# First norm's modulation in columns, from row-wise pieces of the adaptive weights

## The reference, cut to what matters

```
mod = silu(c) @ w_ada + b_ada                 # c: 1024, w_ada: 1024 x 6144
sh1, sc1, gt1, sh2, sc2, gt2 = split(mod, 6)  # 1024 each
u = rmsnorm(x, norm_mix_g) * (1 + sc1) + sh1  # x: 512 tokens x 1024
z = u @ w_in                                  # to the RWKV part, the attention, the gates
... h = x + gt1 * (merged @ w_out) ...        # then norm, 32-expert MoE, final norm
```

## Time and profile before

| | us |
|---|---|
| median of 3 runs | 1351.78 (1351.62 to 1358.64) |
| the profiled execution's own time | 1352.31 |
| its span in the trace | 1350.6 |
| TensorE busy | 1123.2 (83%) |
| VectorE, ScalarE, GpSimd busy | 408.1, 217.7, 164.9 |
| TensorE's granted clock, mean | 0.925 |

### The profile page before, as it was taken

How to read it: one execution, slowest core, us unless ns; L and a number is a source line. 1 busy time by engine, 2 the same in 40 slices (tenths; PEclk the granted TensorE clock), 3 DMA queues, 4 the chain that set the end, 5 groups by cost and what they waited for, 6 DMA issues and landing times. The chain is left out here.

```text
span 1350.6 us, 16451 instructions
## 1 busy us (share of the span) xinstructions
PE 1123.2 (83%) x7001; PEld 572.5 (42%) x7001; DVE 408.1 (30%) x694; ACT 217.7 (16%) x443; POOL 164.9 (12%) x235
## 2 busy tenths in 40 slices
PE   2699999999997887989799992988887877777780
PEld 0343344544465555979644461333332333333330
DVE  4524436632004444345522336110001101111004
ACT  2101123220003452334200120000000000000002
POOL 1100001114001343214100001001000000000002
PEclk9999999879998998999999985988989899998985
DMA  9512326244224003300082445899999999999985
GB/s 341 214 66 94 119 99 242 103 169 125 101 94 133 1 1 120 140 2 4 1 319 110 199 170 216 355 428 427 430 429 429 429 430 429 428 431 428 430 344 202
DMA packets 61345, 311.87 MB, mean 231 GB/s; under 512 B 6194, under 2 KB 12676, under 8 KB 48728
## 3 DMA queue, kind: packets, MB, share of 16 engines
q1 hardware_dynamic: 49784, 273.79, 50.7%
q0 software_dynamic: 9184, 32.82, 6.3%
q10 hardware_dynamic: 2304, 4.20, 0.8%
HBM read 285.11 MB, written 24.64 MB: 229 GB/s over the span
## 5 line engine op out<-in xcount | busy, mean ns | idle before, releaser
L2272 PE MATMUL ps<-ring,zrT 128*64 128x512 f32 x704 | 168.7, 635 | 31.3 <-issue 28.4
L868 PE MATMUL ps<-ring,uT 128*128 128x512 f32 x384 | 169.5, 598 | 1.2 <-PE ps L868 0.6
L2292 PE MATMUL ps<-ring,hdT 128*64 128x512 f32 x352 | 122.2, 633 | 10.4 <-issue 8.5
L859 PE MATMUL ps<-uT,ring 128*128 128x512 f32 x256 | 113.9, 602 | 1.3 <-ACT uT L294 0.7
L2272 PEld LDWEIGHTS ps<-ring,zrT 128*64 128x64 f32 x704 | 57.7, 146 | 133.2 <-issue 132.8
L868 PEld LDWEIGHTS ps<-ring,uT 128*128 128x128 f32 x384 | 72.2, 191 | 92.9 <-issue 92.9
L2097 DVE TENSOR_TENSOR zrT<-zrT,ps 128x512 f32<-128x512 f32 x16 | 11.0, 687 | 290.0 <-PE ps L2272 290.0
L2272 PE MATMUL ps<-mg,zrT 128*64 128x512 f32 x160 | 75.7, 628 | 7.8 <-issue 7.8
L1920 ACT ACTIVATE zrT<-ps 128x512 f32<-128x512 f32 x16 | 9.6, 597 | 422.6 <-PE ps L2272 422.6
L859 PEld LDWEIGHTS ps<-uT,ring 128*128 128x128 f32 x256 | 48.4, 192 | 66.3 <-issue 65.2
L1854 POOL DMA_DIRECT2D y_dram<-zrT x16 | 9.1, 569 | 452.9 <-DVE zrT L2106 452.9
(11 more groups left out here) (365 smaller groups left out, 1478.4 us busy)
## 6 DMA issues: line engine op xcount, KB each, us to landing
ring<-in_moe_w_gate_dram SPq DMA_DIRECT2D x22, 2048.0 KB, 31.3
ring<-in_moe_w_up_dram SPq DMA_DIRECT2D x22, 2048.0 KB, 34.0
ring<-in_moe_w_down_dram SPq DMA_DIRECT2D x22, 2048.0 KB, 33.6
ring<-in_w_ada_dram SPq DMA_DIRECT2D x12, 2048.0 KB, 9.6
ring<-in_w_in_dram SPq DMA_DIRECT2D x9, 2048.0 KB, 13.8
mod<-in_moe_w_up_dram SPq DMA_DIRECT2D x5, 2048.0 KB, 31.5
mg<-in_moe_w_up_dram SPq DMA_DIRECT2D x5, 2048.0 KB, 30.9
uT<-in_moe_w_down_dram SPq DMA_DIRECT2D x5, 2048.0 KB, 36.5
```

The lines of the kernel that those rows point to most:

```text
L859: ins = pe.matmul(ps[:, n % 4, :], slot(name, KD, w)[:, k, c0:c0 + P], uT[:, k, :], start=(k == 0), stop=(k == KD - 1))
L868: ins = pe.matmul(ps[:, n % 4, :], uT[:, k, P * i:P * i + P], w, start=(k == 0), stop=(k == KD - 1))
L2272: ins = pe.matmul(ps[HALF * r:HALF * r + HALF, "gu".index(kind), :], xgT[:, b % 2, k, HALF * r:HALF * r + HALF], w[r][:, k, :], start=(k = ...
L2292: ins = pe.matmul(ps[HALF * r:HALF * r + HALF, 2 + c, :], hdT[:, j, HALF * r:HALF * r + HALF], w[r][:, j, 512 * c:512 * c + 512], start=(j ...
```

## The change

The order of loads is constants, `x`, then the ring. Units 0 to 3 are now two whole rows k of `w_ada` per partition (2048 columns, 8 KB each), each row a load of its own with its own semaphore; `zr0` comes in two halves of four k. VectorE multiplies a row by `silu(c)` and adds it to `acc1` (2048 columns wide): all of it for even k, only the shift half for odd k. The scale half of odd k goes to TensorE as stationary columns (`column_rows`), and the sums of `acc1` over the partitions too (`column_sums`): shift and scale come out as columns, one value per partition and k, in one PSUM bank. ScalarE scales `x` by the reciprocal root, TensorE transposes it before the modulation is known, and VectorE applies shift and scale to `uT` in place, one k at a time; the first z tile waits for each k.

```diff
-        ada_unit(u)
-    win_unit("zr0", 0, 512)
+        units.append((f"ada{u}", [(0, P, (1, 2 * D), ada[:, 2 * u + h:2 * u + h + 1, 0:2 * D]) for h in range(2)]))
+    units.append(("zr0", [(0, P, (4, 512), win[:, 4 * h:4 * h + 4, 0:512]) for h in range(2)]))
...
@@ SyncE
-                load_units(sp, 0, 2)
                 sp.dma_start(x, ...).then_inc(s_h, 16)
-                load_units(sp, 2, index["w1k"])
+                load_units(sp, 0, index["w1k"])
@@ GpSimd
-                pool.dma_start(grow[:, :], A["norm_mix_g"][0].partition_broadcast(P)).then_inc(s_small, 16)
+                pool.dma_start(gcol[:, :], A["norm_mix_g"][0].rearrange("(p k) -> p k", k=KD)).then_inc(s_small, 16)
+                pool.dma_start(bcol[:, :, :], A["b_ada"][0, 0:2 * D].rearrange("(s p k) -> p s k", s=2, k=KD))\
+                    .then_inc(s_small, 16)
@@ ScalarE
-                n1_root(act, 0, NT)
+                act.wait_ge(x_ms, 1)
+                act.activation(xrt, xms, ACT.Sqrt).then_inc(x_rt, 1)
+                act.wait_ge(x_rs, 1)
+                for i in range(NT):
+                    act.activation(x[:, i, :], x[:, i, :], ACT.Copy, scale=xrs[:, i:i + 1]).then_inc(x_sc, 1)
-                for u in range(4): ... copies of ps to mod
+                for n in range(2 * NT):  # then par
+                    act.wait_ge(x_T, n + 1)
+                    act.activation(uT[...], ps[:, n % 4, :]..., ACT.Copy).then_inc(x_ev, 1)
@@ VectorE
-                for u in range(4):
-                    ada(u)
...
+                for k in range(KD):
+                    dve.wait_ge(s_part[k], 16)
+                    w = slot(f"ada{k // 2}", 2, 2 * D)[:, k % 2, :]
+                    if k == 0:
+                        dve.tensor_scalar(acc1[:, :], w, csil[:, 0:1], None, ALU.mult).then_inc(s_ak, 1)
+                    else:
+                        n = D if k % 2 else 2 * D
+                        dve.wait_ge(s_ak, k)
+                        dve.scalar_tensor_tensor(acc1[:, 0:n], w[:, 0:n], csil[:, k:k + 1], acc1[:, 0:n], ...)
+                    if k == 1: ... mean of squares; wait for the root; reciprocal
...
+                dve.wait_ge(s_modp, 4)
+                link(dve.tensor_tensor(scol[:, :, :], ps[:, 4, 0:2 * KD]..., bcol[:, :, :], ALU.add))
+                link(dve.scalar_tensor_tensor(scol[:, 1, :], scol[:, 1, :], 1.0, gcol[:, :], ALU.add, ALU.mult))
+                dve.sem_inc(s_mod, 4)
+                dve.wait_ge(x_ev, 2 * NT)
+                for k in range(KD):
+                    dve.tensor_scalar(uT[:, k, :], uT[:, k, :], scol[:, 1, k:k + 1], scol[:, 0, k:k + 1], ALU.mult, ALU.add)\
+                        .then_inc(s_u1, 1)
@@ TensorE
+                def column(u, k, lhs, rhs, first, last):
+                    r = slice(HD * (u % 2), HD * (u % 2) + HD)
+                    return pe.matmul(ps[r, 4, KD * (u // 2) + k:KD * (u // 2) + k + 1], lhs, rhs, start=first, stop=last)
+                def column_rows(u):  # waits for s_part[2u+1]
+                    for k in range(KD):
+                        for h in range(2):
+                            ins = column(2 + h, k, w[:, D + 512 * h + k:D + 512 * h + 512:KD], csil[:, 2 * u + 1:2 * u + 2], ...)
+                def ada_back(u):     # waits for s_pk u+1 and s_ak 2u+2, gives the slot back
+                def column_sums(s_): # waits for s_ak 8-s_; 16 products of acc1 with a column of ones
-                for u in range(4): spread_mod(u)
+                for _ in range(6):
+                    pe.matmul(ps[:, 5, :], C("ident"), cst[:, 0:T], start=True, stop=True)
+                pe.wait_ge(s_csil, 1)
+                column_rows(0); ada_back(0)
                 pe.wait_ge(s_par, 96)
+                pe.wait_ge(x_sq, NT)
                 pe.transpose(ps[:, 6, 0:34], parr[:, :], C("ident")[0:34, 0:34]).then_inc(s_parT, 1)
-                for i in range(NT): n1_turned(pe, i)
+                x_turned(0); x_turned(1); column_rows(1); ada_back(1)
+                x_turned(2); x_turned(3); column_rows(2); ada_back(2)
+                column_sums(1); column_rows(3); column_sums(0); ada_back(3)
+                pe.wait_ge(x_ev, 2 * NT)
@@ first z tile
+                        if n == 0:
+                            pe.wait_ge(s_u1, k + 1)
+                            if k % 4 == 0:
+                                pe.wait_ge(s_part[2 * index["zr0"] + k // 4], 16)
```

More of the change, by code:

```diff
@@ L151, in build @@
     for n, (_, parts) in enumerate(units):
-        total[where[n]] += 16 * len(parts)
+        total[where[n]] += 16 * len(parts) if n >= FRONT else 0
         arrived.append(total[where[n]])
@@ L196, in build @@
         s_const = sem("s_const")
+        s_part = [sem(f"s_part{n}") for n in range(2 * FRONT)]
         def ring_slot(s_):
@@ L218, in load_units @@
                     eng.wait_ge(unit_free[where[n]], turn_of[n])
-                for p0, np_, (k, w), src in units[n][1]:
-                    eng.dma_start(ring_slot(where[n])[p0:p0 + np_, 0:k * w].rearrange("p (k n) -> p k n", k=k), src)\
-                       .then_inc(unit_in[where[n]], 16)
+                at_ = 0
+                for m, (p0, np_, (k, w), src) in enumerate(units[n][1]):
+                    landed = s_part[2 * n + m] if n < FRONT else unit_in[where[n]]
+                    eng.dma_start(ring_slot(where[n])[p0:p0 + np_, at_:at_ + k * w].rearrange("p (k n) -> p k n", k=k), src)\
+                       .then_inc(landed, 16)
+                    if n < FRONT:
+                        at_ += k * w
         def warm(pe, n=8):
@@ L336, in build @@
         bada = alloc(stage1, "bada", [12, 512])
+        bcol = alloc(stage1, "bcol", [P, 2, KD])
+        gcol = alloc(stage1, "gcol", [P, KD])
+        scol = alloc(stage1, "scol", [P, 2, KD])
+        n1s = alloc(stage1, "n1s", [P, 4, NT])
         uT = alloc(stage1, "uT", [P, KD, T])
@@ L385, in build @@
         junk1 = ps[:, 6:8, :].rearrange("p b n -> p (b n)")
-        n1_square, n1_mean, n1_root, n1_gain, n1_rows, n1_turned, n1_evacuate, _, n1_ev, _, _, _ = norm_mod(
-            stage1, "n1", x, u1, uT, grow, junk1, 0, 1, False)
+        s_ak, s_pk, s_csil = sem("s_ak"), sem("s_pk"), sem("s_csil")
+        acc1 = early[:, 0:2 * D]
+        x_sq, x_ms, x_rt, x_rs, x_sc, x_T, x_ev, s_u1 = (sem(f"x_{n}") for n in "sq ms rt rs sc T ev u1".split())
+        xss, xms, xrt, xrs = (n1s[:, n, :] for n in range(4))
         ztiles = [("T", f"zr{t // 4}", t, P * (t % 4)) for t in range(ZT_TILES)]
@@ L840, in side_job @@
                     ins.then_inc(w_job, 1)
-                for u in range(4):
-                    spread_mod(u)
+                for _ in range(6):
+                    pe.matmul(ps[:, 5, :], C("ident"), cst[:, 0:T], start=True, stop=True)
+                pe.wait_ge(s_csil, 1)
+                column_rows(0)
+                ada_back(0)
                 pe.wait_ge(s_par, 96)
+                pe.wait_ge(x_sq, NT)
                 pe.transpose(ps[:, 6, 0:34], parr[:, :], C("ident")[0:34, 0:34]).then_inc(s_parT, 1)
[L846 to L849, removed]
+                x_turned(0)
+                x_turned(1)
+                column_rows(1)
+                ada_back(1)
+                x_turned(2)
+                x_turned(3)
+                column_rows(2)
+                ada_back(2)
+                column_sums(1)
+                column_rows(3)
+                column_sums(0)
+                ada_back(3)
+                pe.wait_ge(x_ev, 2 * NT)
+                pe.wait_ge(s_small, 48)
                 pe.wait_ge(s_mod, 5)
                 for n, (kind, name, i, c0) in enumerate(ztiles):
-                    if name:
+                    if name and name != "zr0":
                         need(pe, name)
```

71 lines of the change are left out of this document (47 added, 24 removed).

## The result

| | before | after |
|---|---|---|
| median of four runs of each | 1355.21 us (1351.62 to 1362.19) | 1338.72 us (1337.81 to 1341.28) |
| ratio | | 0.987, 95% interval 0.984 to 0.990 |
| the profiled execution | 1352.31, span 1350.6 | 1341.28, span 1339.5 |
| z starts | 62.22 | 39.52 |
| TensorE's granted clock, mean | 0.925 | 0.91 |

Faster by 1.3%: 16.5 us between the medians, 13 to 22 us by the interval, 11.0 us between the two profiled executions. The forecast of 1331.6 was 7 us too low for the median, its range of 1325 to 1340 held it. At the start everything went better than forecast: z began 22.7 us earlier, where 20.2 were expected. So some of the 22.7 us is missing at the end: 11.6 between the two profiled executions, 6.2 between the medians.

A forecast was written before the change was run, and what follows sets the result against it. TensorE, idle for input until z at 62.22 us, was the bound; last sum 40.9, handovers 0.5 and first scaling 0.55 put z at 42.0, winning 20.2 us: 1331.6 us, own range 1325 to 1336, 8 in 10 for 1325 to 1340.

The forecast's parts named there:

- a batch: 16 fp32 one-column products (32 instructions) on TensorE in `column_rows` or `column_sums`: 2.2 us, bounds 1.4 to 4.0.
- the ring: Load slots that TensorE gives back: no gap for `ada3` or `zr0`; `zr1` at worst some 2 us late, free.
- GpSimd's moved loads: Eight transfers, 0.7 MB, now starting near 32 us: take up to 1.9 us from `zr0`, free by 4.5 us.
- dear batches: Column products on TensorE before z cost near 4.0 us a batch: z at 47 to 52, total 1337 to 1342; 13%.
- rival (d): One-column products into one bank don't overlap on TensorE: 7.7 us a batch, z at 70.1, total 1360; 4%.
- The last sum: End of sums(0) on TensorE, just ahead of z: taken as 40.9 us.
- the bound by data: Ahead of z, sums(1) not before k=6 is done at 33.4, then three batches: 40.0 us.
- The 2.8 us: A TensorE batch at the lower clock, if one-column products don't count as activity; z about 3 us later.
- a shift of that start should move everything behind it: From the first z product at 62.22 us products run almost without gap, so an earlier start moves all later stages.
- Rival (a): Column products dear or stalled by instruction loading in the first 40 us: z at 47 to 52, 1337 to 1342; 13%.
- Rival (c): Start is won but given back behind z by a later wait on an absolute time: 1347 to 1352 us; 6%.
- (b): Loads at the start pay a fixed time, 2.5 us each for four added: z at 50.4, total 1340; 4%.

The follow-up runs named there:

- side_by_side: Changed kernel with a batch's 64 stationary columns as memory neighbours instead of every eighth column, output not valid; 1341.26 us, one run.
- hold_z: Changed kernel with 22 chained VectorE copies ahead of the scaling of `uT`, delaying z; 1348.33 us, ratio 0.995 to the kernel before.
- hold_full: Changed kernel with 50 chained VectorE copies ahead of z, so z starts at 62.64; 1361.34 us, ratio 1.003 to the kernel before.
- keep_merge: Changed kernel with three unread TensorE products ending each of the two stages ahead of merge; 1333.34 us, ratio 0.985; repeated 1336.15 us, 0.986.
- x_late: Changed kernel with `x` loaded between `ada1` and `ada2` and the mean of squares after k=3; 1346.25 us, ratio 0.993 to the kernel before.
- before_keep: Kernel before the change with three unread TensorE products ending each of the two stages ahead of merge; 1355.11 us, ratio 1.000.
- keep_more: keep_merge plus two unread products ending the attention stage and one after `column_sums(0)`; 1335.76 us, ratio 0.986 to the kernel before.

## Why the prediction was right and where it was not

Right: that the start is the only thing won; that `x` lands near 13 (12.33); that VectorE would wait for DMA at each k, with additions of 1.285 and 2.35 us (1.28 and 2.35); k=7 at 33.6 (33.41); a batch at 2.2 us (2.09), between its bounds; the first z product inside 37.6 to 46 (39.52). That the ring and GpSimd's moved loads cost nothing held with little room: `zr0`'s first half, put at 36.3, landed at 37.9, 1.6 us before z, and at 39.4 in side_by_side. The DMA engines were full meanwhile (1.06 from 34 to 36 us), but at 342 GB/s, where 24 to 26 us have 426.

The total came inside the range in part by luck. The forecast's own range was 1325 to 1336, and 1338.72 lies above it, in the part that was added for dear batches, which did not come, and for scatter. The 7.1 us between 1331.6 and 1338.72 have three parts. The base was the median of three executions, 1351.78, and that of four is 1355.21: 3.4 us. The code behind z lost 6.2 us that the sum put at nothing, and the start won 2.5 more than forecast: 3.7 us. Where the chances are added up, 89, 7 and 5 make 101; rival (d) alone is 4.

Off in size, on the good side: z at 39.52 instead of 42.0. The last sum was priced at 40.9 and ended at 38.07 (36.01 + 2.06). `x` was scaled from 19.16 instead of 21.5 (`x` 0.7 us earlier, and ScalarE loaded its table at 17.04, before VectorE's mean, not behind it), so TensorE's queue was through in time and waited 0.89 us for VectorE's k=6. That left the bound by data, which the prediction put at 40.0 and which came 1.9 us lower: k=6 was added by 32.1 instead of 33.4, and the three batches behind it took 5.9 us instead of 6.6. The tail behind them was 1.45 us instead of 1.1. From 28 to 38 us, 8 us of that batches of one moving column, the clock is 0.50. By the Trainium skill's TensorE: Matmul & The Clock Gate, Part 1, activity releases the throttle; at these batches the trace shows no release. The 2.8 us that the prediction drew from it for a batch at the lower level was wrong: with the step of eight a batch takes 2.09 at either level.

Wrong: the first paragraph's step, "a shift of that start should move everything behind it". A shift does, as hold_z and hold_full show with 9.0 of 10.0 and 22.0 of 23.1. But the change is no shift alone. It adds instructions to TensorE, which puts a load boundary where it stalls (2.4 us, shown by the place that moves with the instruction count and by the load in the stall), and the merge stage then starts at the lower clock (4.0, shown by keep_merge). That is 6.4 us, and the medians lack 6.2. The rest of the 11.6 between the two profiles is about 1.5 in the chunk stage, 1.5 in the attention stage, 0.8 in the compression stage and 1.2 in z, all with a lower clock. It is not a fixed cost of the change: hold_full and x_late have the changed code without most of it, and before_keep has the part in z and compression without the change. Rival (a) named instruction loading for the first 40 us, where it did nothing visible; the stall sits 490 us further on. Rival (c) had part of the outcome at 6%: 6 us were given back, not nearly all, as its 1347 to 1352 has it, and not by waits on an absolute time. (b) and (d) are refuted by the landings and by the batch of 2.09.

Open: why the changed kernels lose the clock in merge and the kernel before, with gaps of the same 3.5 us, in neither of two profiles. It is not when z starts, as hold_full shows; that the chunk stall shifts what follows by 2.4 us against something is a guess. A kernel that moves the boundary out of the chunk stage was not run. That full DMA queues delay the load would fit its start just as they empty, but the kernel before has a load that goes through among full ones, and no run has them empty: argued, not shown.

## What to carry to other kernels

A saving at the start of a chain of full stages did arrive at the end here, but check it stage by stage: cut both traces at the same work and compare length and clock, before looking for slack. Compare the profiled executions with the medians first; here they made the loss look twice its size. Work added to a long unrolled queue costs at its own place and can cost again far behind, where instruction loads fall; delaying the changed kernel until its lead is gone separates the two. Where the trace shows the lower clock behind a gap of 3 us on TensorE, filling the gap with products that nobody reads is worth a try: it gave 4 us here, 1 us of merge in keep_more, and nothing in the kernel before, which did not have the loss.

## What the hardware showed that was not expected

- A weight load of 64 columns that lie eight elements apart, with a product of one column, goes at 2.09 / 32 = 0.065 us at either clock; of 64 neighbours at 1.10 / 32 = 0.034 with the clock at 1.00 and 1.88 / 32 = 0.059 at 0.50. L826, neighbours too, had 0.041. The row I took as the nearest lacked the step.
- Such products did not raise the clock: nearly gapless batches from 32 to 38 us, clock 0.50 throughout.
- The clock column reads 1.00 for the first 62 us of the kernel before, where L785 runs at half pace (2.08 for two, 1.02 later); before the first change in a trace it is no reading. The pace of a known product is.
- A load of instructions for TensorE, one for about every 250, can come late and cost 1.8 to 2.5 us in a dense stretch; it did at one boundary of the chunk stage, in all eleven profiles of the changed code.
